# Expert down products from fp32r parts in a two-layer mixture-of-experts trunk

## The reference, cut to what matters

```python
def grouped_moe(h, w_router, b_router, w_gate, w_up, w_down):     # once a layer, DEPTH = 2
    ...                                                           # top-2 of 16 experts per token
    hg = jnp.einsum('td,edf->tef', h2, w_gate)                    # t=512, d=1024, e=16, f=256
    hu = jnp.einsum('td,edf->tef', h2, w_up)
    act = jax.nn.silu(hg) * hu * gate_dense[:, :, None].astype(h2.dtype)
    y = jnp.einsum('tef,efd->td', act, w_down)                    # the down products
    return y.reshape(B, S, D)

def reference(x, ...):
    for i in range(DEPTH):
        mix = swa_sink_attention(...) if i % 2 == 0 else forgetting_attention(...)
        x = layer_norm(ALPHA * x + mix, ln_gain[i, 0], ln_bias[i, 0])
        ffn = grouped_moe(x, w_router, b_router, w_gate[i], w_up[i], w_down[i])
        x = layer_norm(ALPHA * x + ffn, ln_gain[i, 1], ln_bias[i, 1])
    return x
```

## Time and profile before

| | us |
|---|---|
| median of 3 runs | 953.28 |
| lowest and highest | 950.37 and 957.61 |
| the profiled execution's own time | 953.39 |
| its span (first to last instruction) | 951.6 |
| its mean granted TensorE clock | 0.981 |
| expert stages (layer 0, layer 1), about | 235 to 403, 741 to 909 |

### The profile page before, as it was taken

How to read it: one execution, slowest core, us unless ns; L and a number is a source line. 1 busy time by engine, 2 the same in 40 slices (tenths; PEclk the granted TensorE clock), 3 DMA queues, 4 the chain that set the end, 5 groups by cost and what they waited for, 6 DMA issues and landing times.

```text
span 951.6 us, 12318 instructions
## 1 busy us (share of the span) xinstructions
PE 892.7 (94%) x4438; PEld 624.3 (66%) x4438; DVE 539.7 (57%) x1098; ACT 376.7 (40%) x755; POOL 125.6 (13%) x137
## 2 busy tenths in 40 slices
PE   6999999997999999989999999999999999998982
PEld 4887777874656656437878886877885565665531
DVE  4444886557666776474342224665366777666437
ACT  3322886001555556231132225776201455555300
POOL 2000332112010000041000001223011201000031
PEclk9999999998999999999999999999999999999997
DMA  9942000119999999572053223110117999999362
GB/s 323 350 157 85 13 1 1 45 65 320 343 361 347 365 357 373 208 263 91 0 198 113 89 89 112 45 46 26 64 45 283 315 350 363 349 352 371 121 211 88
DMA packets 106853, 183.14 MB, mean 192 GB/s; under 512 B 6496, under 2 KB 72032, under 8 KB 106800
## 3 DMA queue, kind: packets, MB, share of 16 engines
q1 hardware_dynamic: 92864, 132.34, 40.9%
q0 software_dynamic: 9200, 33.33, 10.8%
q10 hardware_dynamic: 4736, 16.78, 4.6%
HBM read 159.60 MB, written 22.84 MB: 192 GB/s over the span
## 4 chain that ended last, share of the span: by engine, by line
PE 87%; DVE 5%; DMA 3%; issue 2%; POOL 1%; ACT 1%; POOLq 0%; SPq 0%; DVEq 0%; ACTq 0%
PE bank L519 17%; PE bank L520 17%; PE bank L521 17%; PE bank L764 12%; PE bank L648 5%; PE bank L614 4%; PE bank L631 3%; PE bank L733 2%; PE bank L474 2%; PE bank L500 2%; PE bank L488 1%; DMA arena<-ys,pos 1%; PE bank L683 1%; PE bank L656 1%; DMA ring<-in_swa_w_in 1%
## 5 line engine op out<-in xcount | busy, mean ns | idle before, releaser
L1272 DVE TENSOR_TENSOR low<-ring,gu_high 128x1024 fp32r<-128x1024 f32 x128 | 151.2, 1221 | 55.8 <-ACT gu_high L960 55.8
L960 ACT CAST gu_high<-ring 128x1024 fp32r<-128x1024 f32 x128 | 127.7, 1048 | 21.4 <-DVE arena L1407 16.1
L764 PE MATMUL bank<-ring,arena 128*96 128x512 f32 x256 | 118.3, 606 | 7.3 <-issue 5.0
L519 PE MATMUL bank<-gu_high,rows_high 128*96 128x512 f32 x256 | 113.4, 443 | 2.5 <-DVE rows_low L1391 2.5
L520 PE MATMUL bank<-low,rows_high 128*96 128x512 f32 x256 | 101.9, 398 | 0.0
L521 PE MATMUL bank<-gu_high,rows_low 128*96 128x512 f32 x256 | 101.3, 396 | 0.0
L764 PEld LDWEIGHTS bank<-ring,arena 128*96 128x96 f32 x256 | 39.6, 164 | 62.9 <-issue 62.8
L908 ACT ACTIVATE arena<-arena,nmax 128x256 f32<-128x256 f32 (+3 forms) x128 | 66.8, 522 | 30.9 <-DVE nmax L1203 20.2
L519 PE MATMUL bank<-high,x_high 128*128 128x512 f32 x160 | 65.3, 408 | 6.8 <-DVE low L1099 5.3
L422 POOL TENSOR_TENSOR low<-ring,high 128x512 fp32r<-128x512 f32 x32 | 40.6, 1270 | 231.9 <-ACT high L928 231.9
L648 PE MATMUL bank<-arena 128*128 128x64 f32 x544 | 68.1, 269 | 0.2 <-ACT arena L922 0.2
(11 more groups left out here) (207 smaller groups left out, 1475.7 us busy)
## 6 DMA issues: line engine op xcount, KB each, us to landing
ring<-in_w_gate SPq DMA_DIRECT2D x32, 1024.0 KB
ring<-in_w_up SPq DMA_DIRECT2D x32, 1024.0 KB
ring<-in_w_down SPq DMA_DIRECT2D x32, 1024.0 KB, 14.6
ys<-arena ACTq DMA_DIRECT2D x32, 384.0 KB
ring<-in_fox_w_in SPq DMA_DIRECT2D x6, 2048.0 KB
ring<-in_swa_w_in SPq DMA_DIRECT2D x3, 2048.0 KB
ring<-in_swa_w_o SPq DMA_DIRECT2D x2, 2048.0 KB
xd<-xres ACTq DMA_DIRECT2D x8, 512.0 KB, 2.7
```

Source lines behind the costliest of these rows:

```text
L519: eng.matmul(out, ah, wh, start=(c == 0), stop=False)
L764: mm = eng.matmul(bank[5 + half][0:CAP, :], hT[:, b, c, :], w[:, c, half * BLK:(half + 1) * BLK], start=(c == 0), stop=(c == FC - 1))
L960: eng.copy(gu_high[u % 2][:, part, :], slot_in(use)[:, part, :]).then_inc(S("gu_high"), 1)
L1272: eng.tensor_tensor(lows[use % RING][:, part, :], slot_in(use)[:, part, :], gu_high[u % 2][:, part, :], ALU.subtract).then_inc(S("gu_low"), 1)
```

## The change

The down products of experts 0 to 14 of each layer are made of fp32r parts as gate and up are: three products instead of one fp32 product, for each of two halves and two chunks. The down weight's high part is cast by ACT in two halves of 128x1024 into `d_high`, one buffer for all experts, which lies in `lnp`. Its low part is subtracted by POOL in two halves. The turned result is split by DVE from PSUM (`hT_high`, `hT_low`). Expert 15 keeps the plain fp32 product. ACT's copy of its half now waits for the first half of the product (`d_half`). The load of the second normalisation's gain and bias moves behind the work on expert 14. Gate and up weights are loaded with eight adjacent rows for each partition (pieces of 8 KB instead of 1 KB), and therefore the rows are turned from every eighth column.

```diff
             def load_gate_up(s, w, e, sem):
-                gu = slot_in(s)
-                eng.dma_start(gu[:, :, 0:F], w_gate[w, e].rearrange("(c p) f -> p c f", p=P)).then_inc(sem, 16)
-                eng.dma_start(gu[:, :, F:2 * F], w_up[w, e].rearrange("(c p) f -> p c f", p=P)).then_inc(sem, 16)
+                gu = slot_gate_up(s)
+                eng.dma_start(gu[:, 0, :, :], w_gate[w, e].rearrange("(p c) f -> p c f", p=P)).then_inc(sem, 16)
+                eng.dma_start(gu[:, 1, :, :], w_up[w, e].rearrange("(p c) f -> p c f", p=P)).then_inc(sem, 16)
...
-                if w == 0:
-                    eng.wait_ge(S(f"x_ready{l}{w}"), NT)
-                    load_norm(l, 1)
...
+                def down_low(e):
+                    use = EXP_USE[l] + e
+                    for half in range(2):
+                        cols = slice(half * BLK, (half + 1) * BLK)
+                        eng.wait_ge(S("d_high"), 2 * ((NE - 1) * l + e) + half + 1)
+                        eng.tensor_tensor(d_low[use % RING][:, :, cols], slot_down(use)[:, :, cols],
+                                          d_high[:, :, cols], ALU.subtract).then_inc(S("d_low"), 1)
+                for e in range(RING + 1):
+                    fetch_rows(e)
+                for e in range(NE - 1):
+                    if e + RING + 1 < NE:
+                        fetch_rows(e + RING + 1)
+                    down_low(e)
+                eng.wait_ge(S(f"d_half{l}"), NE - 1)
+                eng.wait_ge(S(f"y_done{l}"), NE - 1)
+                load_norm(l, 1)
...
                 def turn_rows(b):
+                    rows = xe[0:CAP, b, :].rearrange("p (d c) -> p c d", c=KC)
                     for c in range(KC):
-                        mm = eng.transpose(bank[c // 4][:, (c % 4) * P:(c % 4) * P + CAP], xe[0:CAP, b, c * P:(c + 1) * P], ident[0:CAP, 0:CAP])
+                        mm = eng.transpose(bank[c // 4][:, (c % 4) * P:(c % 4) * P + CAP], rows[:, c, :], ident[0:CAP, 0:CAP])
...
+                def down_split(e, b, use):
+                    for half in range(2):
+                        cols = slice(half * BLK, (half + 1) * BLK)
+                        out = bank[5 + half][0:CAP, :]
+                        eng.wait_ge(S("d_low"), 2 * e + (2 * (NE - 1) * l + half + 1))
+                        for c in range(FC):
+                            high, low = d_high[:, c, cols], d_low[use % RING][:, c, cols]
+                            eng.matmul(out, hT_high[:, b, c, :], high, start=(c == 0), stop=False)
+                            eng.matmul(out, hT_high[:, b, c, :], low, start=False, stop=False)
+                            mm = eng.matmul(out, hT_low[:, b, c, :], high, start=False, stop=(c == FC - 1))
+                        if half == 0:
+                            mm.then_inc(S(f"d_half{l}"), 1)
...
+                def down_high(i, u):
+                    use = EXP_USE[l] + u
+                    for half in range(2):
+                        cols = slice(half * BLK, (half + 1) * BLK)
+                        if half == 0:
+                            eng.wait_ge(S(f"d_loaded{use % RING}"), 16 * i + down_count(l, u))
+                        if not isinstance(i, int) or 4 * i + u > 0:
+                            eng.wait_ge(S(f"{('d_half', 'y_done')[half]}{l}"), 4 * i + u)
+                        eng.copy(d_high[:, :, cols], slot_down(use)[:, :, cols]).then_inc(S("d_high"), 1)
                 def evac_y(e, b, stored):
-                    eng.wait_ge(S(f"y_done{l}"), e + 1)
+                    eng.wait_ge(S(f"d_half{l}"), e + 1)
...
                 def step(i, u, first=False, last=False):
                     e = 4 * i + u
+                    if not first:
+                        down_high(i, u - 1)
                     if not first and not last:
                         gate_up_high(i, u + 1, 0, 3)
...
-                    eng.tensor_copy(hT[:, b, :, :], bank[4][:, 0:F]...).then_inc(S("hT_ready"), 1)
+                    h = bank[4][:, 0:F].rearrange("p (c n) -> p c n", c=FC)[:, :, 0:CAP]
+                    if whole:
+                        eng.tensor_copy(hT[:, b, :, :], h).then_inc(S("hT_ready"), 1)
+                    else:
+                        eng.tensor_copy(hT_high[:, b, :, :], h).then_inc(S("hT_high"), 1)
+                        eng.wait_ge(S("hT_high"), e + (1 + (NE - 1) * l))
+                        eng.tensor_tensor(hT_low[:, b, :, :], h, hT_high[:, b, :, :], ALU.subtract).then_inc(S("hT_ready"), 1)
```

More of the change, by code:

```diff
@@ L183, in trunk @@
         lows = [nc.alloc_sbuf_tensor_at(f"low{i}", [P, KC, BLK], fp32r, offset=ring_at + 4 * i * SLOT_WORDS) for i in range(RING)]
+        d_low = [nc.alloc_sbuf_tensor_at(f"d_low{i}", [P, FC, D], fp32r, offset=ring_at + 4 * (i * SLOT_WORDS + KC * BLK)) for i in range(RING)]
+        d_high = nc.alloc_sbuf_tensor_at("d_high", [P, FC, D], fp32r, offset=lnp_at)
+        hT_high = nc.alloc_sbuf_tensor_at("hT_high", [P, 2, FC, CAP], fp32r, offset=arena_at + 4 * 7168)
+        hT_low = nc.alloc_sbuf_tensor_at("hT_low", [P, 2, FC, CAP], fp32r, offset=arena_at + 4 * 9728)
+        gu_low = [nc.alloc_sbuf_tensor_at(f"gu_low{i}", [P, 2, KC, F], fp32r, offset=ring_at + 4 * i * SLOT_WORDS) for i in range(RING)]
         def split(use, pair, c):
@@ L218, in slot_in, with slot_gate_up @@
             return ring[:, k % RING, 0:KC * BLK].rearrange("p (c n) -> p c n", c=KC)
+        def slot_gate_up(k):
+            return ring[:, k % RING, 0:KC * BLK].rearrange("p (g c f) -> p g c f", g=2, c=KC)
         def slot_down(k):
@@ L433, in _, with fetch_rows @@
                 eng.wait_ge(S("ids_ready"), l + 1)
-                for e in range(NE):
+                def fetch_rows(e):
                     if e >= RING:
@@ L745, in gate_up_split @@
                         mm = three(bank[2 + b][0:CAP, :], rows_high[:, b, c, :], rows_low[:, b, c, :],
-                                   gu_high[b][:, c, :], lows[use % RING][:, c, :], c)
+                                   gu_high[b][:, :, c, :], gu_low[use % RING][:, :, c, :], c)
                     return mm
                 def gate_up(b, use):
-                    w = slot_in(use)
+                    w = slot_gate_up(use)
                     for c in range(KC):
-                        mm = eng.matmul(bank[2 + b][0:CAP, :], xeT[:, b, c, :], w[:, c, :], start=(c == 0), stop=(c == KC - 1))
+                        mm = eng.matmul(bank[2 + b][0:CAP, :], xeT[:, b, c, :], w[:, :, c, :], start=(c == 0), stop=(c == KC - 1))
                     return mm
@@ L758, in turn_h, with down @@
                     return mm
-                def down(b, use):
+                def down(b, use, first_half=None):
                     w = slot_down(use)
@@ L765, in down @@
                                             start=(c == 0), stop=(c == FC - 1))
+                        if half == 0 and first_half is not None:
+                            mm.then_inc(first_half, 1)
+                    return mm
+                def down_split(e, b, use):
[10 more added lines that the diff above has]
+                            mm.then_inc(S(f"d_half{l}"), 1)
                     return mm
@@ L788, in down_of @@
                         eng.wait_ge(S("y_dve"), e + NE * l)
-                    down(b, use).then_inc(S(f"y_done{l}"), 1)
+                def down_of(e, b, use, reused):
+                    banks_free(e, reused)
+                    down_split(e, b, use).then_inc(S(f"y_done{l}"), 1)
                 hum(26, 3)
@@ L803, in _ @@
                 turn_h(1).then_inc(S("hT_done"), 1)
-                down_of(NE - 1, 1, EXP_USE[l] + NE - 1, down_count(l, NE - 1), True)
+                use = EXP_USE[l] + NE - 1
+                eng.wait_ge(S(f"d_loaded{use % RING}"), down_count(l, NE - 1))
+                banks_free(NE - 1, True)
+                down(1, use, S(f"d_half{l}")).then_inc(S(f"y_done{l}"), 1)
                 n_ovf = eng.value_load(ovf_id[0:1, OVF:OVF + 1], min_val=0, max_val=OVF)
@@ L959, in gate_up_high @@
                         part = slice(q * PART, (q + 1) * PART)
-                        eng.copy(gu_high[u % 2][:, part, :], slot_in(use)[:, part, :]).then_inc(S("gu_high"), 1)
+                        eng.copy(gu_high[u % 2][:, :, part, :], slot_gate_up(use)[:, :, part, :]).then_inc(S("gu_high"), 1)
                 gate_up_high(0, 0)
@@ L1271, in gate_up_low @@
                         eng.wait_ge(S("gu_high"), SPLITS * 4 * i + (SPLITS * (NE * l + u) + q + 1))
[L1272 to L1273 removed]
+                        eng.tensor_tensor(gu_low[use % RING][:, :, part, :], slot_gate_up(use)[:, :, part, :],
+                                          gu_high[u % 2][:, :, part, :], ALU.subtract).then_inc(S("gu_low"), 1)
                 for t in range(NT):
```

15 lines of the change are left out of this document (7 added, 8 removed).

## The result

| | before | after |
|---|---|---|
| median, us | 952.95 (4 runs) | 1123.1 (4 runs, 1122.71 to 1123.9) |
| span of the profiled execution | 951.6 | 1121.7 |
| mean granted clock | 0.981 | 0.909 |

The ratio is 1.178, with a 95% interval of 1.175 to 1.1809. 1131 was forecast.

The account below looks back on a forecast made before the run. PE was taken to bound the expert stage, with an ACT and DVE chain of the same length beside it. 953.4 plus 2 x 14 x (4.8 + 1.7) = 182, minus 4 for the stall, gave 1131 us; range 1045 to 1175.

Parts of the forecast that it names:

- ACT's casts: Two down-weight casts, 0.98 us each, ahead of gate and up casts in ACT's queue, delay these by 1.96 us, unhidden.
- z: In an expert step, the moment when ACT and DVE begin to copy the results of the last down product.
- The lock: POOL's and DVE's subtractions with two SBUF inputs exclude each other; with ACT's casts and DVE's split, period + 4.8 us.
- The price by proportion, 2.54: POOL's subtraction of a 1024-column half, scaled from 1.27 us for 512 columns; 2.5 was taken.
- The other direction: POOL's subtraction waiting for DVE's, taken from the Trainium skill; with one direction only, the sum would not change.
- The clock: PE idle over 5 us before each down product lowers its clock: 1.69 us more a step, bounds nothing and 2.77.
- Period: Time between down products in the expert stage, forecast to go from 9.98 to 16.5 us, clock included.
- The slack of 0.9 us: Delaying ACT's first gate and up cast by d was said to cost about d - 0.9 us before the down product.
- the rival called faster: Casts and splits hidden if gate and up casts finish less than 0.9 us later; PE alone sets the period: 927, chance 0.05.
- Loads: 8 KB pieces of gate and up weights remove the one stall for a weight: 4.2 us, bounds 0 and 4.2.
- longer transposes: Turning rows from every eighth column on PE: bounds 0 to 1.1 us a step, taken as 0 here.
- The rival without a lock: POOL and DVE do not exclude each other, the ACT and DVE chain remains: 997, or 1045 with the clock; chance 0.12.

Follow-up runs that it names:

- hum_before_down: The changed kernel with 18 useless matmuls more on PE ahead of each split down product: 1069.51 us, ratio 1.1206.
- small_pieces: The changed kernel with gate and up weights in 1 KB pieces and rows turned from adjacent columns again: 1121.73 us, ratio 1.176.
- pool_one_column: The changed kernel with POOL subtracting only one column of each half, PE still making the same 12 matmuls: 1024.95 us, ratio 1.0755.
- the two cuts: On the changed kernel, each alone: POOL's subtractions cut to one column of each half, 1024.95 us; ACT's down casts cut likewise after expert 0, 1096.0 us.
- reordered: The changed kernel with all its work, ACT's and DVE's steps in another order, DVE splitting the turned result first: 960.14 us, ratio 1.0074.
- both_one_column: The changed kernel with both cuts, ACT's down casts and POOL's subtractions reduced to one column of each half: 951.22 us, ratio 0.9968.

## Why the prediction was right

The forecast was 1131 us, 8 above the median, and the mechanism was the forecast one. That it came so near is in part luck, since two terms were off in opposite directions. Point by point:

- **ACT's casts**, z + 1.27, and gate and up casts at z + 3.23: measured z + 1.34 and z + 3.24. DVE ready at z + 4.31: measured 4.31.
- **The lock.** L1210's eight rows were enough to see it. In turn, as walked: POOL, DVE, POOL, DVE, DVE. POOL's halves took 2.41 and 2.22 us of their own instead of 2.5, and DVE's subtractions a little less than walked, so that DVE's chain ended 0.6 earlier and PE began at z + 11.19 instead of z + 11.8. This is the term of the sum that was mis-sized: 0.6 x 28 = 17 us too much. The price by proportion, 2.54, was an upper bound, and the walk took nearly all of it.
- **The other direction**, POOL waiting for DVE, for which the trace of before had no row: the half of 3.34 us shows it. The Trainium skill, "SBUF — State Buffer", section "Who interferes with whom", calls the port that the two engines share an exclusive lock, and says of whichever issues first that it gets it for the whole instruction, in a point on VectorE's two-port modes. This trace agrees in both directions for subtractions with two SBUF inputs: the 3.38 us of DVE and the 3.34 us of POOL.
- **The clock.** 1.7 us a step was assumed from one single event before. The two down products shown lost 2.5 and 1.5 us, and hum_before_down gives 1.9 a step. This was 0.2 x 28 = 6 us too little.
- **Period:** in layer 1 DVE's copies run from 849.94 to 1062.44 in thirteen steps of 16.35 us on the mean, against 16.5 forecast. The sum counts fourteen such steps a layer. The first of them costs less: in layer 0 its copy is at 259.01 instead of 255.61, only 3.4 us later.
- **The slack of 0.9 us** that the prediction reads from the earlier trace rows isn't there. The 3.39 us are ACT's idle time, of which 0.69 are usual. With z at 850.02 the cast of 853.99 came at z + 3.97 instead of z + 1.27, 2.70 late, and PE began its down product at 858.94, z + 8.92 instead of z + 6.23: the delay arrived whole. The sum doesn't use this slack. The condition of the rival called faster does, and was even harder to meet than it says. The row of z:

```profile
850.02 0.69 DVE L1407 COPY arena<-bank 96x512 f32<-96x512 f32 x1 [0.81 <-PE bank L764]
```

- **Loads:** the prediction took 4.2 us off for the stall, which did go, but with its long steps the changed kernel would have lost it with small pieces, too, as the prediction also says: small_pieces was 1.4 us faster than the changed kernel, about as much as the 1.2 us over which the latter's own four runs spread. Without the change's other parts they were worth 5 to 6.5 us, above the bound of 4.2, longer transposes included, whose price, 0.23 a step, was within its bounds of 0 to 1.1.
- **The rival without a lock**, 997 to 1045, is what pool_one_column measured at 1025. The rival that PE alone sets the period did not hold even with both cuts (951, not 927): PE waited for `hT_low` there, which DVE's second operation makes.

The falls of the two cuts do not add up: 98 + 27 is 125, both together 172. A walk along the queues got this right (945 to 958 expected with both cuts). A list of costs by part would not have.

## What to carry to other kernels

Work moved to an idle engine is only free if nobody waits in its place. Look for what it shares, and for an operation in the old trace that is much too long for its size: eight additions of eight columns told here what sixty subtractions would do. With work that is written out in a fixed order, find what stands behind each new operation in its queue before counting busy times: the same work cost 170 us in one order and won 11 in another, of which the loads alone give 5.

## What the runs showed that I had not expected

- The clock fell with only 2.0 us of idle time ahead of each down product (pool_one_column: 894.68 to 898.5, matmuls 0.23 apart at first and 0.43 from 895.94), where 2.5 was the shortest that I had seen in a step before. In reordered, with single waits up to 1.2 us, it stayed at 1.00.
- A weight load for a transpose from every eighth fp32 column takes 205 ns instead of 141, and eight transposes 1.05 instead of 0.82 us.
- POOL needs 2.36 to 2.46 us for 1024 columns where 512 take 1.27, when nothing disturbs it.
- POOL's gathers take 1.71 us in the changed kernel instead of 0.90, and about as much in pool_one_column, but mostly 0.90 in both_one_column. The traces show the cause: DVE's subtractions with two SBUF inputs hold up a gather, too. The gather of 908.24 above began while DVE's second subtraction ran, which ended at 909.17, and it ended 0.78 us after that, at 909.95. In all kept traces, every gather that began while such a subtraction was running ended 0.77 to 0.79 us after it and took 1.48 to 1.95 us, but for two that began within 0.02 us of a subtraction's start; the others took 0.90 to 1.04 us. In the kernel before, no gather fell beside one. Nobody waits for them here.
